# Hybrid decoder step on one core: three rounded products for fourteen half tiles per mixer, and 32x32 diagonal parts in the triangular inverse

## What is computed

```python
def mixer(u, conv_buf, dn_buf, s0, w_in, conv_w, dn_conv_w, a_log, dt_bias, dn_norm_w, w_out):
    p = u @ w_in                                       # 1024 -> 3592 columns
    yc, new_conv_buf = causal_dwconv(gate_c * h_in, conv_buf, conv_w)
    y_conv = gate_b * yc
    qkv, new_dn_buf = causal_dwconv(p[..., OFF_QKV:OFF_Z], dn_buf, dn_conv_w)
    ...
    o, s_new = gated_delta_rule(q, k, v, g, beta, s0)  # needs (I + M)^-1, M strictly lower
    o = o * lax.rsqrt(jnp.mean(o * o, -1, keepdims=True) + RMS_EPS) * dn_norm_w
    o = o.reshape(bsz, t, DN_WIDTH) * jax.nn.silu(z)
    return jnp.concatenate([y_conv, o], -1) @ w_out, new_conv_buf, new_dn_buf, s_new
```

## Time and profile before

| | us |
|---|---|
| median of 3 runs (lowest to highest) | 1363.96 (1362.47 to 1364.56) |
| the profiled execution | 1362.47 |
| its span, first to last instruction | 1360.7 |

### The profile page before, as it was taken

How to read it: one execution, slowest core, us unless ns; L and a number is a source line. 1 busy time by engine, 2 the same in 40 slices (tenths; PEclk the granted TensorE clock), 3 DMA queues, 4 the chain that set the end, 5 groups by cost and what they waited for, 6 DMA issues and landing times.

```text
span 1360.7 us, 21809 instructions
## 1 busy us (share of the span) xinstructions
PE 1316.1 (97%) x9092; PEld 1092.1 (80%) x9092; DVE 812.2 (60%) x1300; ACT 550.3 (40%) x719; POOL 50.7 (4%) x104
## 2 busy tenths in 40 slices
PE   6999999899999999999997999999999999999996
PEld 3678687699999977777785999999967787876673
DVE  1676227564454447751557634644555768999896
ACT  1351113353433224321314533333344546777762
POOL 7000012000000000000300000000000000000000
PEclk8999999999999999999998999999999999999998
DMA  9644856955545453548250934734656768999991
GB/s 317 225 155 166 276 182 218 313 159 161 178 150 163 164 182 93 185 147 261 95 164 14 298 96 146 231 111 139 214 180 222 224 235 289 339 345 357 333 343 38
DMA packets 189942, 275.87 MB, mean 203 GB/s; under 512 B 7816, under 2 KB 136098, under 8 KB 184725
## 3 DMA queue, kind: packets, MB, share of 16 engines
q1 hardware_dynamic: 177856, 263.62, 58.0%
q10 hardware_dynamic: 11988, 10.86, 2.8%
HBM read 268.16 MB, written 6.30 MB: 202 GB/s over the span
## 4 chain that ended last, share of the span: by engine, by line
PE 90%; DVE 5%; DMA 2%; ACT 2%; issue 1%; SPq 1%; ACTq 0%; DVEq 0%
PE bank L1229 14%; PE bank L1015 12%; PE bank L1016 11%; PE bank L1017 11%; PE bank L1045 7%; PE bank L1047 7%; PE bank L1046 7%; PE bank L1085 4%; DMA raw<-in_w_ada_dram 2%; PE bank L1162 2%; PE bank L1603 1%; PE bank L1334 1%; PE bank L1366 1%; PE bank L1370 1%; PE bank L1475 1%
## 5 line engine op out<-in xcount | busy, mean ns | idle before, releaser
L775 DVE TENSOR_TENSOR lo_raw<-raw,hi 128x2048 fp32r<-128x2048 f32 (+2 forms) x112 | 229.3, 2055 | 99.6 <-ACT hi L1851 60.9
L1851 ACT ACTIVATE hi<-raw 128x2048 fp32r<-128x2048 f32 (+2 forms) x112 | 193.3, 1727 | 113.6 <-PE bank L1047 78.3
L1229 PE MATMUL bank<-UM,raw 128*128 128x288 f32 x864 | 219.2, 409 | 0.0
L1015 PE MATMUL bank<-UH,hi 128*128 128x288 f32 x704 | 210.0, 298 | 5.4 <-DVE UL L2264 5.1
L1017 PE MATMUL bank<-UL,hi 128*128 128x288 f32 x704 | 207.6, 295 | 0.0
L1229 PEld LDWEIGHTS bank<-UM,raw 128*128 128x128 f32 x864 | 160.7, 190 | 49.9 <-issue 8.1
L2276 DVE TENSOR_TENSOR lo<-raw,hi 128x2048 fp32r<-128x2048 f32 (+1 forms) x42 | 94.1, 2241 | 83.5 <-ACT hi L2061 48.5
L1015 PEld LDWEIGHTS bank<-UH,hi 128*128 128x128 f32 x704 | 132.7, 188 | 6.6 <-issue 4.9
L1017 PEld LDWEIGHTS bank<-UL,hi 128*128 128x128 f32 x704 | 133.1, 189 | 0.0
L1016 PE MATMUL bank<-UH,lo 128*128 128x288 f32 x432 | 128.0, 296 | 0.0
L1045 PE MATMUL bank<-hi,UGH 128*128 128x512 f32 (+9 forms) x288 | 111.7, 388 | 0.0
(11 more groups left out here) (481 smaller groups left out, 2429.7 us busy)
## 6 DMA issues: line engine op xcount, KB each, us to landing
raw<-in_w_ada_dram SPq DMA_DIRECT2D x48, 1024.0 KB, 6.5
raw<-in_w_in_dram SPq DMA_DIRECT2D x28, 1024.0 KB, 7.7
raw<-in_w_exp_gate_dram SPq DMA_DIRECT2D x26, 1024.0 KB, 5.5
raw<-in_w_exp_up_dram SPq DMA_DIRECT2D x26, 1024.0 KB, 8.0
raw<-in_w_exp_down_dram SPq DMA_DIRECT2D x16, 1024.0 KB, 5.2
raw<-in_w_exp_down_dram SPq DMA_DIRECT2D x16, 768.0 KB, 4.5
raw<-in_w_ff_gate_dram SPq DMA_DIRECT2D x11, 1024.0 KB, 5.5
raw<-in_w_ff_up_dram SPq DMA_DIRECT2D x11, 1024.0 KB, 5.3
```

Source lines behind the costliest of these rows:

```text
L775: dve.tensor_tensor(lo_x[g % XRAW][:, 0:XG[g][2] * XG[g][3]], x_raw(g), hi_x[g % XSPLIT][:, 0:XG[g][2] * XG[g][3]].bitcast(F32), ALU.subtr ...
L1015: pe.matmul(out, wh, xh, start=start, stop=False)
L1229: mm = pe.matmul(bank[t][:, 0:N], w_[:, d, t * P:t * P + P], UM[:, d, :], start=(d == 0), stop=(d == KT - 1))
L1851: act.activation(hi_x[q][:, 0:XG[g][2] * XG[g][3]], x_raw(g), ACT.Copy).then_inc(S("x_hi_made"), 1)
```

## The change

- **Rounded products.** The 14 half tiles (7, 0) to (13, 1) of each layer go through `mm3`. New steps: `uh` (ACT copies the rounded modulated input to UH2), `ul` (DVE puts the rest in UL, over UM), and `ts` for each half tile (ACT copies the rounded weights, 128x1024, to one of six places `home`; DVE writes the rest over the raw block). A `ts` stands one step ahead of the half tile before its own, and that of (13, 0) ahead of (12, 0).
- **Places.** Homes are shared: where one was used before in the layer, ACT's copy waits for the matmuls of that earlier half tile. Half tiles up to the first `wh` alternate between homes 0 and 1. (12, 0) and (13, 0) both have home 3.
- **Diagonal parts.** At levels 2 to 16, X and Y of groups A and B work on 32x32 diagonal blocks of all eight prompt units: A on blocks 0 and 1 (banks 2 and 3), B on blocks 2 and 3 (banks 6 and 7). DVE reads X with four operations of 32x256 and Y with four of 32x512 (T and TT in one). Unit C keeps 128x128 matmuls in bank 5; its second product in Y is dropped.
- **Order.** `sd_in` moves ahead of half tile (6, 0). `wh` and `wl` of the second `w_out` tile move behind `wc`. POOL multiplies by z first and scales the old state afterwards. The convolution state is stored in two parts.

```diff
@@ steps_of
             for _ in range(n):
+                ahead = {(12, 0): fill[1:3], (12, 1): fill[2:3], (13, 0): []}.get(fill[0], fill[1:2])
+                s.extend(('ts', l, *x) for x in ahead if fill[0] >= FIRST3)
                 tile(l, *fill.pop(0))
...
+        one('uh', 'sd_in')
         filler()
         solve('X', 8)
         one('qd')
+        s.append(('ts', l, *FIRST3))
         filler()
         solve('Y', 8)
+        one('ul')
         s.append(('st_out', l, 0))
...
-        s.append(('wh', l, 1))
         filler()
         one('cs_out', 'on')
-        s.append(('wl', l, 1))
         filler()
...
-        s += [('su', l, 0), ('sm', l, 0)]
+        s += [('wh', l, 1), ('su', l, 0), ('sm', l, 0), ('wl', l, 1)]
@@
+def home_of(l, m, t):
+    late = {(12, 1): 4, (13, 0): 3, (13, 1): 5}
+    if (m, t) in late:
+        return late[m, t]
+    i = STEPS.index(('ts', l, m, t))
+    first = next(x for x, s in enumerate(STEPS) if s[:3] == ('wh', l, 0))
+    if i < first and STEPS.index(('pt', l, m, t)) < first:
+        return 2 * m % 2 + t
+    return 2 + (t + 1) % 2
+def diagonal(grp):
+    return [(GRP[grp][y], slice(32 * g, 32 * g + 32)) for y, g in enumerate((0, 1) if grp == 'A' else (2, 3))]
@@ gpsimd
             for l in range(DEPTH):
+                pool.wait_ge(S("o_squared"), l + 1)
+                pool.tensor_tensor(OT[:, :, :], OT[:, :, :], Z[:, :, :], ALU.mult).then_inc(S("o_z"), 1)
                 pool.wait_ge(S("vx_made"), l + 1)
...
-                pool.wait_ge(S("o_squared"), l + 1)
-                pool.tensor_tensor(OT[:, :, :], OT[:, :, :], Z[:, :, :], ALU.mult).then_inc(S("o_z"), 1)
@@ tensor
+                elif k == 'pt' and s[1:] in THREE:
+                    fill(base, t)
+                    pe.wait_ge(S("tile_split"), j + 1)
+                    for d in range(KT):
+                        if s[2:] == FIRST3 and d % 4 == 0:
+                            pe.wait_ge(S("u_low_made"), 2 * l + d // 4 + 1)
+                        mm = mm3(bank[t][:, 0:N], wh[:, d, :], wl[:, d, t * P:t * P + P], UH2[d // 4][:, d % 4, :], UL[:, d, :],
+                                 d == 0, d == KT - 1)
+                    mm.then_inc(full[t], 1)
...
                     if s[2] < 32:
-                        for x, u in enumerate(us):
-                            mm = pe.matmul(bank[b][:, x * P:x * P + P], MT[:, u, :], Tm[:, u, :], start=True, stop=True)
-                        mm.then_inc(full[b], 1)
+                        fill(base, GRP[s[3]][1])
+                        for u in range(DEC):
+                            for b, v in diagonal(s[3]):
+                                mm = pe.matmul(bank[b][v, 32 * u:32 * u + 32], MT[v, u, v], Tm[v, u, v], start=True, stop=True)
...
+                    for u in range(DEC):
+                        for b, v in diagonal(s[3]):
+                            pe.matmul(bank[b][v, 32 * u:32 * u + 32], TTm[v, u, v], X[v, u, v], start=True, stop=True)
+                            mm = pe.matmul(bank[b][v, 32 * (DEC + u):32 * (DEC + u) + 32], X[v, u, v], TTm[v, u, v], start=True, stop=True)
@@ scalar
+                elif k == 'uh':
+                    act.wait_ge(full[2], base[2])
+                    for h in range(2):
+                        act.activation(UH2[h][:, :, :], UM[:, 4 * h:4 * h + 4, :], ACT.Copy).then_inc(S("u_hi_made"), 1)
+                elif k == 'ts':
+                    act.wait_ge(S(f"raw_full{n_ % RAW}"), 16 * (n_ // RAW + 1))
+                    if used:
+                        act.wait_ge(full[used[-1][2]], TILE_FULL[used[-1]])
+                    act.activation(home[HOMES[j]][:, :, :], src, ACT.Copy).then_inc(S("tile_hi"), 1)
@@ vector
+                elif k == 'ul':
+                    dve.wait_ge(full[1], TILE_FULL[l, 6, 1])
+                    for h in range(2):
+                        dve.tensor_tensor(UL[:, 4 * h:4 * h + 4, :], UM[:, 4 * h:4 * h + 4, :], UH2[h][:, :, :].bitcast(F32),
+                                          ALU.subtract).then_inc(S("u_low_made"), 1)
+                elif k == 'ts':
+                    dve.wait_ge(S("tile_hi"), j + 1)
+                    dve.tensor_tensor(part(lo_x[slot][:, :]), part(raw[:, slot, :]), home[HOMES[j]][:, :, :].bitcast(F32),
+                                      ALU.subtract).then_inc(S("tile_split"), 1)
+                elif k == 'X' and s[2] < 32:
+                    for b, v in diagonal(s[3]):
+                        got(base, b)
+                        dve.tensor_tensor(X[v, 0:DEC, v], bank[b][v, 0:32 * DEC].rearrange("p (u t) -> p u t", u=DEC),
+                                          rep(lev[s[2]][v, v], 1, DEC), ALU.mult).then_inc(read[b], 1)
+                elif k == 'Y' and s[2] < 32:
+                    for b, v in diagonal(s[3]):
+                        got(base, b)
+                        both = Tboth[v, :, 0:DEC, v]
+                        dve.tensor_tensor(both, both, bank[b][v, :].rearrange("p (x u t) -> p x u t", x=2, u=DEC),
+                                          ALU.subtract).then_inc(read[b], 1)
```

More of the change, by code:

```diff
@@ L415, in banks_of @@
         return one(2, 3, 6)
+    if k in 'XY' and step[3] == 'C':
+        return one(5)
     if k == 'X':
-        return one(*GRP[step[3]][:2 if step[2] == 32 else 1])
+        return one(*GRP[step[3]][:1 if step[2] == 64 else 2])
     if k == 'Y':
@@ L481, in half_of @@
     return (m + 1) % SPLIT
+THREE = [s[1:] for s in STEPS if s[0] == 'ts']
+TILE_FULL = {}
+_f = [0] * 8
+for _s in STEPS:
+    for _b, _k in banks_of(_s).items():
+        _f[_b] += _k
+    if _s[0] == 'pt':
+        TILE_FULL[_s[1:]] = _f[_s[3]]
+def home_of(l, m, t):
[7 more added lines that the diff above has]
+    return 2 + (t + 1) % 2
+HOMES = [home_of(*x) for x in THREE]
 LOADS = []
@@ L1325, in step @@
                         mm.then_inc(full[b], 1)
+                elif k == 'X' and s[3] == 'C':
+                    fill(base, 5)
+                    pe.matmul(bank[5][:, 0:P], MT[:, DEC, :], Tm[:, DEC, :], start=True, stop=True).then_inc(full[5], 1)
+                elif k == 'Y' and s[3] == 'C':
+                    fill(base, 5)
+                    pe.matmul(bank[5][:, 0:P], X[:, DEC, :], TTm[:, DEC, :], start=True, stop=True).then_inc(full[5], 1)
                 elif k == 'X':
@@ L1360, in step @@
                 elif k == 'Y':
-                    b, bt, us = GRP[s[3]]
-                    pe.wait_ge(read[b], base[b])
-                    if s[2] < 64:
+                    for b, _ in diagonal(s[3]):
                         fill(base, b)
[L1365 to L1371, removed]
+                    for u in range(DEC):
+                        for b, v in diagonal(s[3]):
+                            pe.matmul(bank[b][v, 32 * u:32 * u + 32], TTm[v, u, v], X[v, u, v], start=True, stop=True)
+                            mm = pe.matmul(bank[b][v, 32 * (DEC + u):32 * (DEC + u) + 32], X[v, u, v], TTm[v, u, v], start=True, stop=True)
+                            if u == DEC - 1:
+                                mm.then_inc(full[b], 1)
                 elif k == 'wt':
@@ L1969, in step @@
                     act.activation(w(112), w(32), ACT.Exp, scale=-1.0).then_inc(S("gate_exps"), 1)
[L1970 to L1971 removed]
+                    act.wait_ge(S("gate_exps"), 2 * l + 1)
+                    act.activation(w(128), w(112), ACT.Ln, bias=eps[:, 2:3]).then_inc(S("gate_exps"), 1)
                 elif k == 'gx':
```

105 lines of the change are left out of this document (69 added, 36 removed).

## The result

| | us |
|---|---|
| before, median of 6 runs (lowest to highest) | 1362.99 (1362.47 to 1364.56) |
| after, median of 6 runs (lowest to highest) | 1371.3 (1368.78 to 1380.69) |
| ratio, 95% interval | 1.0068 (1.0045 to 1.0092) |
| after, the profiled execution; its span | 1372.55; 1370.8 |

The change made the kernel slower by 0.7%. The prediction was 1347 and faster: it is wrong in sign, and the time lies 13 us above its range. The gains came as counted, and a little larger. Two costs that the sum had at nothing ate them: a lower clock of PE behind its waits, short ones too, and pauses in the supply of PE's instructions.

The account below looks back on a forecast made before the run. PE, 97% busy and nearly gapless, was taken as the bound. 35.1 us less and 18.0 back gave net 17.1: 1345.4 for the profiled execution, a median of about 1347 us. Range 1333 to 1358; faster 0.91.

Parts of the forecast that it names:

- Part 1: Rounded half tiles as three products: 3.18 us each for 3.88, 28 half tiles, 19.6 us less.
- Part 2: 32x32 blocks in X and Y, eight levels, and C's dropped second product: 14.4 us less; uncovered DVE gives 3.7 back.
- Rival 4: Y of levels 2 to 16 gains nothing, taking 3.8 us a level: 1358 us; chance 0.09.
- The rule of program order: Matmuls start and end in order, only weight loads pulled ahead; read as making Y take 3.8 us a level.
- 128 products, 2.4 us: New Y at levels 2 to 16: 128 instructions, PE time 2.4 us a level, 1.2 less than before.
- Part 3: Earlier load of the state: tile 9's wait goes, 1.1 us less; split waits at (9, 0) and (9, 1), 1.8 back.
- Part 4: End of the mixer: PE waits 5.5 us in layer 1, 5.6 more in layer 0, 1.4 elsewhere; 12.5 us back.
- rival 2: PE's clock falls behind the two new waits of 5.5 us, costing 2 to 3 us, up to 8: 1350 to 1355; chance 0.10.
- the two long waits: PE's waits at the output norm's `sp`, one per layer: 5.5 us in layer 1, 6.3 in layer 0.
- Its argument against: Against a falling clock: layer 0 held a clock of 1.00 through its 1.1 us wait.
- nearly hidden: DVE's reads of Y at levels 2, 8 and 16, where other work of PE follows.

Follow-up runs that it names:

- diag_only: The kernel before with only the 32x32 diagonal blocks on levels 2 to 16, nothing rounded, no load or tile moved: 1356.4 us, ratio 0.9958.
- diag64: The kernel before with 64x64 diagonal blocks for X and Y on levels 2 to 16, nothing rounded: 1351.6 us, ratio 0.9915.
- stalls: The kernel before with PE held four times in each layer's mixer by short POOL writes, nothing else changed: 1388.5 us, ratio 1.0180.
- warm_sp: The changed kernel with products of constants into an idle bank ahead of PE's wait for the output norm: 1363.7 us, ratio 1.0008.
- round_only: The changed kernel with the 128x128 products back on levels 2 to 16, rounding and the new order kept: 1368.2 us, ratio 1.0039.

## Why the prediction was wrong

- **Part 1** (19.6 less): right. Half tiles follow each other in 3.19 us at full clock, 3.18 predicted. ACT's copies of after (start us, us), each released by the end of a half tile:

```profile
171.18 1.06 ACT L2007 ACTIVATE home<-raw 128x1024 fp32r<-128x1024 f32 x1 [2.96 <-PE bank L1066]
...
174.37 1.06 ACT L2007 ACTIVATE home<-raw 128x1024 fp32r<-128x1024 f32 x1 [2.13 <-PE bank L1066]
```

- **Part 2** (14.4 less): the work was sized a little too high. X takes 1.1 us and Y 2.0, for 1.2 and 2.4 predicted: 8 x (0.1 + 0.4) = 4 more gained, 18 in all. Rival 4 (Y at 3.8) is refuted: 128 products of 32 columns on four places run at 16 ns each. The rule of program order, which the prediction took from the Trainium skill, is not refuted by this, but was misread: matmuls that start and end in order can still overlap, as these do (each 0.25 us long, 16 ns apart), so it never gave 3.8. What failed is the step "128 products, 2.4 us": it counted the array's time and not that PE needs 256 instructions in 2 us. Level 32, the row it went by, has half as many and shows no pause. It did not ask either what the DMA queues carried while the blocks of instructions came. 6.9 us, at nothing in the sum.
- **Part 3** (0.7 back in all): the splits of (9, 0) and (9, 1) were predicted to make PE wait 1.1 and 0.7 us; it waited 2.6 and nothing. Its weights were expected 2.6 us sooner than before and landed at 163.6, 4 us sooner, but PE too was earlier. A small miss.
- **Part 4** (12.5 back): the mechanism and the size were right. In layer 1, (12, 0) ended on PE at 671.05, P; the broadcast was counted for P + 13.4 and started at 684.50, P + 13.45. PE was there at P + 8.35 for 7.85. The chain reads as written, DVE's subtraction for (13, 0) ahead of the convolution of (12, 0):

```profile
671.26 1.06 ACT L2007 ACTIVATE home<-raw 128x1024 fp32r<-128x1024 f32 x1 [8.51 <-PE bank L1066]
...
672.36 1.56 DVE L2583 TENSOR_TENSOR lo_raw<-raw,home 128x1024 fp32r<-128x1024 f32 x1 [1.44 <-ACT home L2007]
673.84 0.37 DVE L2491 TENSOR_SCALAR YTM<-CH,pT 128x304 f32<-128x304 f32 x1
...
684.50 1.34 PE L1332 MATMUL bank<-RBO,ones 1*128 1x288 f32 x8 [5.10 <-ACT RBO L1942]
```

  Layer 0 waited 7.7 us for 6.3. Where it said that layer 1 would hardly be touched by POOL it was wrong. DVE's subtraction for (11, 1) took 2.83 us there, beside POOL, for 1.22, and PE waited 2.4 us for it, 1.1 predicted. The Trainium skill's rule on two SBUF inputs ("SBUF — State Buffer", Who interferes with whom) holds for this subtraction too; the prediction applied it to `c2` and the convolution alone.
- **The clock** (nothing in the sum; rival 2 at 2 to 3 us, 8 at most, chance 0.10): this is the step that failed most, by about 20 us: some 13 in the account's stretches and 6.4 behind the two long waits. Rival 2 named the mechanism and priced it for two waits of 5.5 us. It left out that a wait of 1 to 3 us can be followed by a dip too, and that the sum itself added some ten waits of 0.1 to 1.2 us, of which the longest came out at 2.6. Its argument against, that layer 0 held 1.00 through a 1.1 us wait, was one draw: the same 1.1 us wait ahead of level 2 in layer 0 is followed by a clock of 0.71 in after and of 1.00 in `diag_only` and `diag64`. The waits that it listed as "nearly hidden" or as a few tenths were priced at their length alone.
- In sum: 17.1 us less were forecast, and the profiled span is 10.1 longer, 27 us off (24 by the medians): about 20 for the clock, 7 for the pauses, 3 for larger waits, less 4 for the inverse; about 1 is left.
- **The range and the chances.** Faster had 0.91. The range took its bounds from the sizes of the parts, and every bound assumed full clock. With `stalls` in hand, the new waits of 1 to 3 us would have been given 0.4 to 2 us each on top, and the two long ones at least 2.

## What to carry to other kernels

On a kernel whose PE has no gaps, a new wait of PE costs its length and often about half as much again in clock behind it (8 us on 17.2 in `stalls`); count the waits that a change adds, not only their sum, and fill a wait that can't be removed with idle products (7.6 us here). Packing work into many small instructions saves array time only as far as instructions arrive, and the longest pauses came while bulk loads filled the DMA engines: twice as large blocks at half the count took PE the same time, and the kernel came out 4.8 us faster. Where a split is made just in time by two other engines, what stands between it and its half tile on each queue decides, and the gain of rounding (19.6 us) was nearly all spent there.

## What was not expected of the hardware

- PE's clock fell behind waits as short as 1.1 us, but not each time: one of four waits of 1.3 to 1.4 us and four of four of 2.9 to 3.0 us in `stalls`. The dips lasted some 3 to 10 us, with windows of 5 us down to 0.50.
- Kernels with many such waits mostly spread: 1368.8 to 1380.7 for after and 1359.9 to 1368.5 for `warm_sp`, against 1351.0 to 1352.6 for `diag64`. Not all do: `round_only`, with both long waits, had 1367.2 to 1368.4.
- PE paused for 0.5 to 3.4 us in the kernels with runs of 128 instructions of 32 columns. With 64 of 64 columns two of four kernels had a pause, of 0.4 and 2.5 us. Each pause ended 1.2 to 1.8 us after a block of instructions had landed.
- 32-column products on four places ran at 16 ns each, 64-column ones at 30 ns, so both took 2.0 us a level.
